# A fused two-block kernel: sparse attention's rotary half swap, by a TensorE permutation or by transfers within SBUF

## The chip, the cores and the metric

One Trainium2 chip, one core of it. The time is device microseconds of one execution of the whole program; lower is better. All arithmetic is in fp32 (with fp32r pairs for the large products).

## What is computed

The program runs a first block (two layers with a short convolution, a WKV recurrence and MLPs) and then a second block (sparse attention A, MLP, forgetting attention B, MLP) on 256 tokens of width 1024. The change touches sparse attention A alone:

```python
def apply_rope(x):                     # x: heads of 64
    half = d // 2
    x1, x2 = x[..., :half], x[..., half:]
    return concatenate([x1 * c - x2 * sn, x1 * sn + x2 * c], axis=-1)

def dsa_attention(xn, w_in, w_o):
    q, k, v, qi, ki, wi = split(xn @ w_in)
    q, k, qi, ki = (apply_rope(t) for t in (q, k, qi, ki))
    idx_logits = einsum('bqhd,bsd->bqhs', qi, ki)
    score = einsum('bqhs,bqh->bqs', relu(idx_logits), wi)      # admissible keys only
    sel = top_k(score, 64)
    logits = q @ k[sel] / 8;  o = softmax(logits) @ v[sel]
    return o @ w_o
```

## The kernel before

Everything is feature-major: 128 features on the partitions (two heads of 64), 256 tokens along the row. A large product is cut into weight units of 1 MB (1024 x 256, or 512 x 512 for the output weights). SP loads a unit into one of four `stage` buffers; ScalarE copies it to `w_hi` (fp32r), and VectorE or GpSimd subtracts to make `w_lo` (each in two halves, two buffers of each); TensorE then makes three products per tile (lines 2259 to 2261, or 2316 to 2318 for the wide units). SP's queue is one in-order list of transfers: the load of unit u waits until unit u-4 has both its `w_lo` halves (`lo_made`).

The units of attention A are numbered here from 0: 0 is the index key with its head weights, 1 and 2 the index queries, 3 the key, 4 the value, 5 to 8 the queries Q0 to Q3, 9 to 12 the output weights; after them come the units of the next MLP. `w_lo` of units 6, 7 and 8 is made by GpSimd (line 860, eight instructions each), that of the others by VectorE (line 1514).

The rotary embedding runs on eight results r = 0 to 7: the index key (one tile of 256 tokens), two index queries, the key, Q0 to Q3 (two tiles each). For each, ScalarE copies the unit's PSUM bank to `rope_in[r % 2]` (line 1366, which frees the bank, `un_free`). TensorE multiplies it with a 128 x 128 signed permutation `rot_w`, so that each half of a head comes to stand where the other was (lines 2781 and 2853); GpSimd makes the cosine product `rope_c` (line 850); VectorE makes the sine product from PSUM (line 2058) and adds `rope_c` (line 2060, `rope_done`). `rope_c` is one buffer, so GpSimd's cosine product of r waits for the sum of r-1.

The order on each engine is written out by hand. GpSimd's list has, after the rotary product of r = 3, 4 and 5, the subtraction of unit 6, 7 and 8, and each of these waits for the sum of that r (`rope_done`). VectorE's list is: index sums, scores(0), `w_lo` of unit 5, scores(1), the key's sum, half of the selection of 64 keys, Q0's sum, the other half of the selection, `sel_bias`, the first pair of heads' logits, Q1's sum, then a loop over eight pairs p with Q2's sum in p = 1 and Q3's in p = 3; `w_lo` of unit 9 is made in p = 2. TensorE's logits of pair p wait for the sum of Q(p // 2), from the fifth pair on (p >= 5) for all four sums.

Of the kernel before, what the change touches and what calls it, by code (L numbers as in the profile page):

```python
# [7 lines left out]
ALU = mybir.AluOpType  # L8
# [5 lines left out]
P = 128  # L14
# [6 lines left out]
HD = 64  # L21
# [27 lines left out]
CONST_PARTS = ((("ident", P), ("mean", P), ("ones", P), ("rot", P)),  # L49
# [13 lines left out]
def constant_table():  # L63
# [13 lines left out]
    rot = np.zeros((P, P))  # L77
    for m in range(P):
        d = m % HD
        rot[m + HD // 2 if d < HD // 2 else m - HD // 2, m] = -1.0 if d < HD // 2 else 1.0  # L80
    put("rot", rot)
# [11 lines left out]
    put("sin", np.tile(np.sin(ang), (4, 1)))  # L93
# [7 lines left out]
def build(nc, A, out):  # L101

    with ExitStack() as ctx:
# [65 lines left out]
        ident, mean_w, ones_w, head_ones, head_mean, rot_w = (c_(n) for n in ("ident", "mean", "ones", "head_ones", "head_mean", "rot"))  # L169
# [105 lines left out]
        rope_in = [at(f"rope_in{i}", [P, 2, SEQ], r_off[3] + 2048 * i) for i in range(2)]  # L275
        rope_c = at("rope_c", [P, 2, SEQ], r_off[3] + 4096)
# [185 lines left out]
        ROPE_KI, ROPE_QI, ROPE_K, ROPE_Q, N_ROPE = 0, 1, 3, 4, 8  # L462

# [164 lines left out]
        def _(sp):  # L628
# [29 lines left out]

            for k in range(ADA_FIRST):
                sp.dma_start(ada_buf[ada_slot(k)][:], ada_src(k)).then_inc(ada_first_landed[k], 16)  # L660
                if k == 0:
                    sp.dma_start(vec_in[:, 0:2, :], A["vec_table"][0:2 * P].rearrange("(t r) q -> r t q", r=P)).then_inc(vec_loaded, 16)
                    sp.dma_start(vec_in[0:N_VEC - 2 * P, 2, :], A["vec_table"][2 * P:]).then_inc(vec_loaded, 16)
                    sp.dma_start(const[0][:], A["const_table"][:, CONST_AT[0]:CONST_AT[1]]).then_inc(const_in, 16)
                if k == 1:
                    sp.dma_start(x[:], A["x"][0].rearrange("(a p) d -> p a d", p=P)).then_inc(x_loaded, 16)
            for u in range(NU):
# [59 lines left out]
        rot_done, rope_done, ki_copied, cos_done, kdup_ready = (sem(n) for n in ("rot_done", "rope_done", "ki_copied", "cos_done", "kdup_ready"))  # L727
# [9 lines left out]
        def _(pool):  # L737
# [107 lines left out]
            for r in range(N_ROPE):  # L845
                n = 1 if r == ROPE_KI else 2
                pool.wait_ge(un_free, freed(V_A + ROPE_USE[r]))
                if r:
                    pool.wait_ge(sem("rope_done"), r)
                G.tensor_tensor(rope_c[:, 0:n, :], rope_in[r % 2][:, 0:n, :], cos_root.unsqueeze(1).to_broadcast([P, n, SEQ]), ALU.mult)\  # L850
                    .then_inc(sem("cos_done"), 1)
# [640 lines left out]
        def _(dve):  # L1492
# [650 lines left out]
            dve.wait_ge(rot_done, ROPE_KI + 1)  # L2143
# [14 lines left out]
            def rope_query(j):  # L2158
                rope(ROPE_Q + j, 2, q_fm[:, 2 * j:2 * j + 2, :], un[(V_A + 5 + j) % 2])
# [3 lines left out]
            V.tensor_scalar(sel_bias[:], score[:], 0.5 * TAKEN, NEG, ALU.is_gt, ALU.mult).then_inc(sem("keys_chosen"), 1)  # L2163
            dve.wait_ge(sem("keys_chosen"), 1)
# [89 lines left out]
        def _(pe):  # L2254
# [630 lines left out]
            rot(ROPE_K, 2, V_A + 3)  # L2885
# [3 lines left out]
            rot_query(0)  # L2889
# [5 lines left out]
            rot_query(1)  # L2895
# [3 lines left out]
            for p in range(1, PAIRS):  # L2899
# [5 lines left out]
                if p in (1, 3):  # L2905
                    rot_query(p // 2 + 2)
# [128 lines left out]
```

## Time and profile before

| | us |
|---|---|
| median of 3 runs | 1351.86 (1350.39 to 1352.41) |
| the profiled execution: its own time | 1350.53 |
| its span, first to last instruction | 1348.8 |
| TensorE matmul busy | 1303.3 (97%) |
| VectorE busy | 948.8 (70%) |
| ScalarE busy | 701.5 (52%) |
| GpSimd busy | 128.3 (10%) |
| HBM, mean over the span | 189 GB/s |

Busy is the time in which an engine executed an instruction, added over the span. Attention A's projections and heads take the stretch from about 755 to 850 us. PE is TensorE, DVE VectorE, ACT ScalarE, POOL GpSimd, SPq the transfers that SP issues.

### The profile page before, as it was taken

What the parts mean: (1) busy time and instruction counts of PE and PEld (TensorE: products, weight loads), DVE (VectorE), ACT (ScalarE), POOL (GpSimd) and SP (SyncE); (2) the same over time, 40 slices, a digit from 0 to 9 for tenths busy, and PEclk for the clock granted to TensorE, in tenths of its full rate; (3) what the DMA queues carried; (4) which work ended last, traced back from release to release, by engine and by line L of the source; (5) the groups of instructions that cost most, each with busy time, mean ns of one, the idle gap of its engine ahead of it and who ended that gap; (6) DMA issues with size and microseconds to landing.
All of it is one profiled execution on the core that took longest, in us unless ns stands there. A gap on an engine that the chain in (4) does not pass through costs nothing. (4 is left out here: it accounts for less than half of the span.)

```text
span 1348.8 us, 24952 instructions
## 1 busy us (share of the span) xinstructions
PE 1303.3 (97%) x10507; PEld 1129.8 (84%) x10507; DVE 948.8 (70%) x1433; ACT 701.5 (52%) x1211; POOL 128.3 (10%) x133
## 2 busy tenths in 40 slices
PE   4999999999999999999999999999999999999997
PEld 2998888998899897788888887888888998888886
DVE  1887788976768776675566888666656677756655
ACT  2544544434567555564444648654445566644443
POOL 0000000010200764100000042000000021000000
PEclk9999999999999999999999999999999999999999
DMA  9996799995341012356665532465555543565561
GB/s 362 372 363 237 299 356 380 352 343 167 115 156 64 4 35 97 95 176 201 188 189 176 182 113 91 148 206 192 187 190 160 174 139 126 172 188 194 183 197 50
DMA packets 177575, 256.90 MB, mean 190 GB/s; under 512 B 10488, under 2 KB 122552, under 8 KB 177464
## 3 DMA queue, kind: packets, MB, share of 16 engines
q1 hardware_dynamic: 177464, 255.31, 56.8%
q8 instruction: 83, 1.36, 0.4%
q14 instruction: 28, 0.23, 0.1%
HBM read 254.25 MB, written 1.05 MB: 189 GB/s over the span
## 5 line engine op out<-in xcount | busy, mean ns | idle before, releaser
L1514 DVE TENSOR_TENSOR w_lo<-stage,w_hi 128x1024 fp32r<-128x1024 f32 (+1 forms) x372 | 447.6, 1239 | 160.4 <-ACT w_hi L889 160.0
L889 ACT ACTIVATE w_hi<-stage 128x1024 fp32r<-128x1024 f32 (+1 forms) x378 | 380.1, 1049 | 211.7 <-PE acc L2318 191.9
L2316 PE MATMUL acc<-w_hi,z_hi 128*128 128x512 f32 x640 | 252.6, 395 | 1.6 <-DVE z_lo L1963 1.6
L2318 PE MATMUL acc<-w_hi,z_lo 128*128 128x512 f32 x640 | 249.4, 390 | 0.0
L2317 PE MATMUL acc<-w_lo,z_hi 128*128 128x512 f32 x640 | 249.2, 389 | 0.0
L2259 PE MATMUL un<-h_both,w_hi 128*128 128x256 f32 x736 | 214.3, 291 | 1.8 <-POOL w_lo L860 1.1
L2260 PE MATMUL un<-h_both,w_hi 128*128 128x256 f32 x736 | 208.1, 283 | 0.0
L2261 PE MATMUL un<-h_both,w_lo 128*128 128x256 f32 x736 | 208.0, 283 | 0.0
L2259 PEld LDWEIGHTS un<-h_both,w_hi 128*128 128x128 f32 x736 | 140.8, 191 | 9.5 <-issue 5.4
L2316 PEld LDWEIGHTS acc<-w_hi,z_hi 128*128 128x128 f32 x640 | 120.1, 188 | 27.8 <-issue 4.0
L2260 PEld LDWEIGHTS un<-h_both,w_hi 128*128 128x128 f32 x736 | 141.0, 192 | 1.2 <-issue 0.7
L2318 PEld LDWEIGHTS acc<-w_hi,z_lo 128*128 128x128 f32 x640 | 120.1, 188 | 25.4
L2261 PEld LDWEIGHTS un<-h_both,w_lo 128*128 128x128 f32 x736 | 140.9, 191 | 0.0
L2317 PEld LDWEIGHTS acc<-w_lo,z_hi 128*128 128x128 f32 x640 | 120.3, 188 | 23.5
L2297 PE MATMUL un<-h_both,w_hi 128*128 128x512 f32 x384 | 121.2, 397 | 0.4 <-DVE w_lo L1514 0.4
L2297 PE MATMUL side<-h_both,w_hi 128*128 128x512 f32 x384 | 120.8, 396 | 0.4
L2300 PEld LDWEIGHTS side<-h_both,w_lo 128*128 128x128 f32 x384 | 72.1, 188 | 17.0
L2300 PEld LDWEIGHTS un<-h_both,w_lo 128*128 128x128 f32 x384 | 72.1, 188 | 16.9
L2300 PE MATMUL un<-h_both,w_lo 128*128 128x256 f32 x384 | 75.5, 278 | 0.0
L2300 PE MATMUL side<-h_both,w_lo 128*128 128x256 f32 x384 | 75.4, 278 | 0.0
L1796 DVE SCALAR_TENSOR_TENSOR ada_sum<-ada_buf,small,ada_sum 128x1024 f32<-128x1024 f32 x49 | 62.8, 1282 | 1.0
L2297 PEld LDWEIGHTS un<-h_both,w_hi 128*128 128x128 f32 x384 | 59.1, 189 | 1.6 <-DVE w_lo L1514 0.6
(393 smaller groups left out, 1886.0 us busy)
## 6 DMA issues: line engine op xcount, KB each, us to landing
stage<-in_mlp_w SPq DMA_DIRECT2D x64, 1024.0 KB
ada_buf<-in_ada_w SPq DMA_DIRECT2D x48, 1024.0 KB, 11.4
stage<-in_w_up SPq DMA_DIRECT2D x32, 1024.0 KB
stage<-in_w_down SPq DMA_DIRECT2D x32, 1024.0 KB
stage<-in_conv_w_in SPq DMA_DIRECT2D x12, 1024.0 KB
stage<-in_rw_w_rkv SPq DMA_DIRECT2D x12, 1024.0 KB
stage<-in_w_in_a SPq DMA_DIRECT2D x8, 1024.0 KB
stage<-in_w_kv_b SPq DMA_DIRECT2D x8, 1024.0 KB
```

What stands on the lines that cost most here:

```text
L889: A_(w_hi[u % 2][:, half, 0:n], stage[u % NSTAGE][:, half, 0:n], ACT.Copy).then_inc(hi_made, 1)
L1514: V.tensor_tensor(w_lo[u % 2][:, half, 0:n], stage[u % NSTAGE][:, half, 0:n], w_hi[u % 2][:, half, 0:n].bitcast(F32), ALU.subtract).then_i ...
L1796: V.scalar_tensor_tensor(out=to[:], in0=rows, scalar=by, in1=to[:], op0=ALU.mult, op1=ALU.add).then_inc(ada_weighed, 1)
L2259: MM(out, hi_l, hi_r, start=start, stop=False, skip_group_check=True)
L2260: MM(out, hi_l, lo_r, start=False, stop=False, skip_group_check=True)
L2261: return MM(out, lo_l, hi_r, start=False, stop=stop, skip_group_check=True)
L2297: MM(pair[:, m, :, :], wh[:, kt, c], h_both[:, kt, :, :], start=(kt == 0), stop=False, skip_group_check=True)
L2300: ins = MM(pair[:, m, 0, :], wl[:, kt, c], h_hi[:, kt, :], start=False, stop=(kt == KT - 1), skip_group_check=True)
L2316: MM(y, z_hi[:, kt, q], wh[:, i, :], start=(first and kt == 0), stop=False, skip_group_check=True)
L2317: MM(y, z_hi[:, kt, q], wl[:, i, :], start=False, stop=False, skip_group_check=True)
L2318: ins = MM(y, z_lo[:, kt, q], wh[:, i, :], start=False, stop=(last and kt == KT - 1), skip_group_check=True)
```

## The change

The half swap is no longer made by TensorE. SP issues, for each r, four transfers from `rope_in` to a new buffer `rope_turned[r % 2]` of 32 partitions each, block 0 to 1, 1 to 0, 2 to 3 and 3 to 2, as soon as `rope_in` is there. GpSimd makes the cosine product and behind it the sine product in place on `rope_turned`; the sign is in the sine table now. VectorE only adds the two. The eight permutation products, the wait of TensorE's later units for the sums, and the separate semaphore behind `sel_bias` are gone. The new buffer lies in the second half of `tmp`.

In SP's list the swaps stand at fixed places, each ahead of one weight load: r = 0 to 3 ahead of the loads of units 6 to 9, r = 4 ahead of unit 11, r = 5 ahead of unit 12, r = 6 and 7 ahead of the next MLP's first and second unit (`SWAPPED_AHEAD`).

```diff
-    put("sin", np.tile(np.sin(ang), (4, 1)))
+    put("sin", np.tile(np.sin(ang), (4, 1)) * np.where(i % HD < HD // 2, -1.0, 1.0)[:, None])
...
+        rope_turned = [at(f"rope_turned{i}", [P, 2, SEQ], tmp_off + 4096 + 2048 * i) for i in range(2)]
...
+        SWAPPED_AHEAD = (U_KI + 6, U_KI + 7, U_KI + 8, U_KI + 9, U_QA + 6, U_QA + 7, U_OA + 4, U_OA + 5)
...
+            def swap_halves(r):
+                n = 1 if r == ROPE_KI else 2
+                sp.wait_ge(un_free, freed(V_A + ROPE_USE[r]))
+                for g in range(4):
+                    to, src = 32 * g, 32 * (g ^ 1)
+                    sp.dma_start(rope_turned[r % 2][to:to + 32, 0:n, :], rope_in[r % 2][src:src + 32, 0:n, :]).then_inc(sem(f"rope_landed{r % 2}"), 16)
...
+                if u in SWAPPED_AHEAD:
+                    swap_halves(SWAPPED_AHEAD.index(u))
                 load_unit(u)
...
-                G.tensor_tensor(rope_c[:, 0:n, :], rope_in[r % 2][:, 0:n, :], cos_root.unsqueeze(1).to_broadcast([P, n, SEQ]), ALU.mult)\
-                    .then_inc(sem("cos_done"), 1)
+                G.tensor_tensor(rope_c[:, 0:n, :], rope_in[r % 2][:, 0:n, :], cos_root.unsqueeze(1).to_broadcast([P, n, SEQ]), ALU.mult)
+                pool.wait_ge(sem(f"rope_landed{r % 2}"), 64 * (r // 2 + 1))
+                turned = rope_turned[r % 2][:, 0:n, :]
+                G.tensor_tensor(turned, turned, sin_root.unsqueeze(1).to_broadcast([P, n, SEQ]), ALU.mult).then_inc(sem("cos_done"), 1)
...
-            def rope(r, n, dst, bank=misc):
-                dve.wait_ge(rot_done, r + 1)
-                link(V.tensor_tensor(dst, bank[:, 0:n, :], bc4(sin_root, n), ALU.mult))
+            def rope(r, n, dst):
                 dve.wait_ge(cos_done, r + 1)
-                V.tensor_tensor(dst, dst, rope_c[:, 0:n, :], ALU.add).then_inc(rope_done, 1)
+                V.tensor_tensor(dst, rope_turned[r % 2][:, 0:n, :], rope_c[:, 0:n, :], ALU.add).then_inc(rope_done, 1)
...
-            def rot(r, n, v):
-                pe.wait_ge(un_free, freed(v))
-                if r:
-                    pe.wait_ge(rope_done, r)
-                MM(misc[:, 0:n, :], rot_w, rope_in[r % 2][:, 0:n, :], start=True, stop=True).then_inc(rot_done, 1)
...
             def a_unit(k, tokens=False):
                 free_bank(V_A + k)
-                if k >= 7:
-                    pe.wait_ge(rope_done, ROPE_Q + k - 6)
...
-            def rot_query(j):
-                v = V_A + 5 + j
-                pe.wait_ge(un_free, freed(v))
-                MM(un[v % 2][:], rot_w, rope_in[(ROPE_Q + j) % 2][:], start=True, stop=True).then_inc(rot_done, 1)
```

How the lists stand around the queries. SP's list before, from the load of unit 8 (the first row) over units 9 to 12 to the first two units of the next MLP:

```order
L644 DMA stage_49<-in_w_in_a 128x8x256 [waits lo_made]
L644 DMA stage_50<-in_w_o_a 128x4x512 [waits lo_made]
L644 DMA stage_51<-in_w_o_a 128x4x512 [waits lo_made]
L644 DMA stage_52<-in_w_o_a 128x4x512 [waits lo_made]
L644 DMA stage_49<-in_w_o_a 128x4x512 [waits lo_made]
L644 DMA stage_50<-in_w_up 128x8x256 [waits lo_made]
L644 DMA stage_51<-in_w_up 128x8x256 [waits lo_made]
```

And now, from the load of unit 10 to the last swap (Q0 to Q3 are `rope_in_161`, `162`, `161`, `162`):

```order
L641 DMA stage_51<-in_w_o_a 128x4x512 [waits lo_made]
L662 DMA rope_turned_163<-rope_in_161 32x512 [waits un_free]
L662 DMA rope_turned_163<-rope_in_161 32x512 x3
L641 DMA stage_52<-in_w_o_a 128x4x512 [waits lo_made]
L662 DMA rope_turned_164<-rope_in_162 32x512 [waits un_free]
L662 DMA rope_turned_164<-rope_in_162 32x512 x3
L641 DMA stage_49<-in_w_o_a 128x4x512 [waits lo_made]
L662 DMA rope_turned_163<-rope_in_161 32x512 [waits un_free]
L662 DMA rope_turned_163<-rope_in_161 32x512 x3
L641 DMA stage_50<-in_w_up 128x8x256 [waits lo_made]
L662 DMA rope_turned_164<-rope_in_162 32x512 [waits un_free]
L662 DMA rope_turned_164<-rope_in_162 32x512 x3
```

Each swap of a query stands directly behind a weight load: Q0's behind unit 10, Q1's behind unit 11, Q2's behind unit 12, Q3's behind the next MLP's first unit, and these four loads wait for `w_lo` of units 6, 7, 8 and 9.

GpSimd's list before, from Q0's cosine product over the subtraction of unit 7 to Q1's:

```order
L850 TENSOR_TENSOR rope_c<-rope_in_161,rstd 128x512 [waits rope_done,un_free]
L860 TENSOR_TENSOR w_lo_56<-stage_52,w_hi_54 128x256 [waits hi_made,lo_made,rope_done]
L860 TENSOR_TENSOR w_lo_56<-stage_52,w_hi_54 128x256 x3
L860 TENSOR_TENSOR w_lo_56<-stage_52,w_hi_54 128x256 [waits hi_made]
L860 TENSOR_TENSOR w_lo_56<-stage_52,w_hi_54 128x256 x3
L850 TENSOR_TENSOR rope_c<-rope_in_162,rstd 128x512 [waits rope_done,un_free]
```

And the same stretch now:

```order
L857 TENSOR_TENSOR rope_c<-rope_in_161,rstd 128x512 [waits rope_done,un_free]
L860 TENSOR_TENSOR rope_turned_163<-rope_turned_163,rstd 128x512 [waits rope_landed0]
L869 TENSOR_TENSOR w_lo_56<-stage_52,w_hi_54 128x256 [waits hi_made,lo_made,rope_done]
L869 TENSOR_TENSOR w_lo_56<-stage_52,w_hi_54 128x256 x3
L869 TENSOR_TENSOR w_lo_56<-stage_52,w_hi_54 128x256 [waits hi_made]
L869 TENSOR_TENSOR w_lo_56<-stage_52,w_hi_54 128x256 x3
L857 TENSOR_TENSOR rope_c<-rope_in_162,rstd 128x512 [waits rope_done,un_free]
L860 TENSOR_TENSOR rope_turned_164<-rope_turned_164,rstd 128x512 [waits rope_landed1]
```

The sine product has joined the cosine product, with a wait for the swap's landing between them; the subtraction of the weight unit stands behind both, as it stood behind the one.

## Rows read from the trace of the kernel before

**Rows 1.** the page, its part on busy time per engine
```profile
PE 1303.3 (97%) x10507; PEld 1129.8 (84%) x10507; DVE 948.8 (70%) x1433; ACT 701.5 (52%) x1211; POOL 128.3 (10%) x133
```

**Rows 2.** windows (us; busy us of each engine with instruction counts; TensorE clock; DMA)
```profile
795.00:810.00 15.00, 14.31 (x108) 12.28 (x108) 13.80 (x45) 8.04 (x13) 11.23 (x15) 1.00 0.40 133
...
830.00:840.00 10.00, 10.00 (x78) 7.62 (x78) 8.41 (x18) 8.73 (x27) 0.00 (x0) 1.00 0.01 2
```

**Rows 3.** timeline of PE: start, duration, line, operands; the second rotary product
```profile
771.49 0.28 PE L2261 MATMUL un<-h_both,w_lo 128*128 128x256 f32 x1
771.61 1.02 PE L2781 MATMUL side<-rope_in,const 128*128 128x512 f32 x2
...
772.59 0.28 PE L2260 MATMUL un<-h_both,w_hi 128*128 128x256 f32 x1
```

**Rows 4.** timeline of DVE; in brackets the idle time before, its releaser
```profile
773.40 0.69 DVE L2060 TENSOR_TENSOR qi_fm<-qi_fm,rope_c 128x512 f32<-128x512 f32 x1
774.01 3.43 DVE L1514 TENSOR_TENSOR w_lo<-stage,w_hi 128x1024 fp32r<-128x1024 f32 x2
...
786.85 0.48 DVE L2123 SCALAR_TENSOR_TENSOR score<-score_r,wi_tok,const 128x256 f32<-128x256 f32 x1 [0.37 <-ACT score_r L1385]
...
791.75 0.69 DVE L2060 TENSOR_TENSOR kA_fm<-kA_fm,rope_c 128x512 f32<-128x512 f32 x1
...
799.48 0.69 DVE L2060 TENSOR_TENSOR q_fm<-q_fm,rope_c 128x512 f32<-128x512 f32 x1 [0.68 <-POOL rope_c L850]
...
819.20 0.69 DVE L2060 TENSOR_TENSOR q_fm<-q_fm,rope_c 128x512 f32<-128x512 f32 x1
...
822.51 2.35 DVE L1514 TENSOR_TENSOR w_lo<-stage,w_hi 128x1024 fp32r<-128x1024 f32 x2
...
828.22 0.69 DVE L2060 TENSOR_TENSOR q_fm<-q_fm,rope_c 128x512 f32<-128x512 f32 x1
```

**Rows 5.** the rotary products on POOL: min/median/max ns, first and last start
```profile
L850 POOL TENSOR_TENSOR rope_c<-rope_in,rstd x8: 746/1285/2122, 769.8 to 826.4; 128x512 f32<-128x512 f32 x7, 128x256 f32<-128x256 f32 x1
```

**Rows 6.** timeline of POOL
```profile
774.23 2.12 POOL L850 TENSOR_TENSOR rope_c<-rope_in,rstd 128x512 f32<-128x512 f32 x1 [1.68 <-DVE qi_fm L2060]
...
792.53 5.59 POOL L860 TENSOR_TENSOR w_lo<-stage,w_hi 128x256 fp32r<-128x256 f32 x8 [11.31 <-DVE kA_fm L2060]
```

**Rows 7.** timeline of SP's queue, one of the weight loads
```profile
798.15 0.39 SPq L644 DMA_DIRECT2D stage<-in_w_o_a  x1
```

**Rows 8.** who SP's queue waited for, 755 to 850 us: total, times, longest
```profile
SPq L644 <- POOL w_lo L860: 29.0, 3, 11.2
```

**Rows 9.** windows of the load issued at 798.15 us, DMA share and GB/s last
```profile
801.70:802.70 1.00, 1.00 (x11) 0.87 (x10) 0.96 (x6) 0.11 (x1) 1.00 (x2) 1.00 0.89 344
802.70:803.70 1.00, 1.00 (x11) 0.67 (x10) 0.93 (x5) 0.98 (x2) 1.00 (x2) 1.00 0.03 10
```

**Rows 10.** tiles: four 32-partition pieces of lora_g2b, and the output's four
```profile
L681 SPq DMA_DIRECT2D lora_g2b<-in_rw_g x4: 417/421/429, 335.9 to 337.3; - x4
...
DMA to landing us min/median/max: 3.9/4.1/4.4
...
DMA to landing us min/median/max: 2.0/2.1/2.1
```

**Rows 11.** timeline of PE, the index scores and the logits of the fifth pair
```profile
779.15 1.16 PE L2838 MATMUL acc<-ki_fm,qi_fm 64*128 64x128 f32 x16
...
828.96 0.93 PE L2792 MATMUL un<-k_dup,q_fm 64*128 64x128 f32 x8 [0.43 <-DVE q_fm L2060]
```

**Rows 12.** PE near the start of the run, one timeline row and three windows
```profile
16.20 0.91 PE L2326 MATMUL acc<-const,xs_sq 128*128 128x128 f32 x3 [7.23 <-DVE xs_sq L1537]
...
20.60:22.80 2.20, 2.20 (x25) 1.06 (x28) 0.00 (x0) 0.00 (x0) 0.00 (x0) 1.00 1.03 411
22.80:25.00 2.20, 2.20 (x28) 1.06 (x24) 0.00 (x0) 0.00 (x0) 0.00 (x0) 1.00 1.03 410
25.00:27.20 2.20, 2.20 (x48) 1.23 (x44) 0.00 (x0) 0.38 (x1) 0.00 (x0) 1.00 1.01 399
```

More of the change, by code:

```diff
@@ L45 @@
            "c", "final_g", "g_attn_a_2", "g_kv_2", "g_attn_b_2", "g_mlp_2", "g_final_2")
-CONST_PARTS = ((("ident", P), ("mean", P), ("ones", P), ("rot", P)),
+CONST_PARTS = ((("ident", P), ("mean", P), ("ones", P), ("still", P)),
                (("head_ones", P), ("head_mean", P), ("level_t", 6 * CHUNK), ("masks", 2 * CHUNK), ("eye", CHUNK), ("resets", SEQ),
@@ L76, in constant_table @@
     put("head_mean", same_head / HD)
[L77 to L81, printed above, removed]
     s, q = i[:, None] % CHUNK, np.arange(CHUNK)[None, :]
@@ L167, in c_ @@
             return const[i][:, lo - CONST_AT[i]:hi - CONST_AT[i]]
-        ident, mean_w, ones_w, head_ones, head_mean, rot_w = (c_(n) for n in ("ident", "mean", "ones", "head_ones", "head_mean", "rot"))
+        ident, mean_w, ones_w, head_ones, head_mean = (c_(n) for n in ("ident", "mean", "ones", "head_ones", "head_mean"))
         level_t = c_("level_t").rearrange("p (j q) -> p j q", j=6)
@@ L726, in build @@
                              "bonus_gated", "weighed", "scaled", "group_done", "last_done"))
-        rot_done, rope_done, ki_copied, cos_done, kdup_ready = (sem(n) for n in ("rot_done", "rope_done", "ki_copied", "cos_done", "kdup_ready"))
+        wi_turned, rope_done, ki_copied, cos_done, kdup_ready = (sem(n) for n in ("wi_turned", "rope_done", "ki_copied", "cos_done", "kdup_ready"))
         score_done, score_relu, score_used = sem("score_done"), sem("score_relu"), sem("score_used")
@@ L2142, in _ @@
             dve.wait_ge(tables_made, 1)
-            dve.wait_ge(rot_done, ROPE_KI + 1)
+            dve.wait_ge(wi_turned, 1)
             for a in range(QT):
@@ L2158, in rope_query @@
             def rope_query(j):
-                rope(ROPE_Q + j, 2, q_fm[:, 2 * j:2 * j + 2, :], un[(V_A + 5 + j) % 2])
+                rope(ROPE_Q + j, 2, q_fm[:, 2 * j:2 * j + 2, :])
             rope_query(0)
             select(rounds - rounds // 2)
-            V.tensor_scalar(sel_bias[:], score[:], 0.5 * TAKEN, NEG, ALU.is_gt, ALU.mult).then_inc(sem("keys_chosen"), 1)
-            dve.wait_ge(sem("keys_chosen"), 1)
+            link(V.tensor_scalar(sel_bias[:], score[:], 0.5 * TAKEN, NEG, ALU.is_gt, ALU.mult))
             pair_logits(0, 0)
@@ L2844, in a_half @@
                     free_bank(V_A + k)
-                    if k >= 7:
-                        pe.wait_ge(rope_done, ROPE_Q + k - 6)
                 unit(U_KI + k, un[(V_A + k) % 2], h_tiles, tokens=tokens, kts=HALVES[n])
-            def rot_query(j):
-                v = V_A + 5 + j
-                pe.wait_ge(un_free, freed(v))
-                MM(un[v % 2][:], rot_w, rope_in[(ROPE_Q + j) % 2][:], start=True, stop=True).then_inc(rot_done, 1)
             def a_products(p):
@@ L2874, in _ @@
             for a in range(QT):
-                nc.tensor.transpose(misc[:, 1, IDX_HEADS * a:IDX_HEADS * (a + 1)], rope_in[ROPE_KI % 2][HD:KI_COLS, 0, P * a:P * a + P],
+                ins = nc.tensor.transpose(misc[:, 1, IDX_HEADS * a:IDX_HEADS * (a + 1)], rope_in[ROPE_KI % 2][HD:KI_COLS, 0, P * a:P * a + P],
                                     ident[HD:KI_COLS, HD:KI_COLS])
-            rot(ROPE_KI, 1, V_A)
+            ins.then_inc(wi_turned, 1)
             a_unit(2)
-            rot(ROPE_QI, 2, V_A + 1)
             a_half(3, 0)
-            rot(ROPE_QI + 1, 2, V_A + 2)
             a_half(3, 1)
@@ L2884, in _ @@
             a_half(4, 0, tokens=True)
-            rot(ROPE_K, 2, V_A + 3)
             index_scores(1)
@@ L2888, in _ @@
             a_unit(5)
-            rot_query(0)
             a_unit(6)
@@ L2894, in _ @@
             a_half(7, 0)
-            rot_query(1)
             a_products(1)
@@ L2904, in _ @@
                 pair_turns(0, p - 1)
-                if p in (1, 3):
-                    rot_query(p // 2 + 2)
                 if p in (1, 2):
```

## The prediction

> **What bounds the kernel now.** The page's first part says that TensorE is the bound over the whole span: 1303.3 us busy, 97% [rows 1]. The change sits in one stretch, so the windows come next. From 795 to 810 us, where the keys are selected and Q0 and Q1 are turned, PE is busy 14.31 of 15 us and VectorE 13.80; from 830 to 840 PE is busy 10.00 of 10 [rows 2]. So a microsecond taken from TensorE is gained only where nothing else is late, and any lateness that reaches 830 us is carried to the end, for from there PE has no gap to lose it in. Third, the timelines of VectorE, GpSimd and SP tell who is right behind whom. Q0's sum waited 0.68 us for GpSimd's product [rows 4]; the logits of pair p = 5 started at 828.96 after 0.43 us of waiting for Q3's sum [rows 11], which ends at 828.22 + 0.69 = 828.91 [rows 4]. The rotary sums are thus already at the edge of the path. Fourth, SP: its queue waited 29.0 us, three times, for GpSimd's `w_lo` [rows 8]. The load at 798.15 [rows 7] is that of unit 10, and it went out when GpSimd had ended unit 6, at 792.53 + 5.59 = 798.12 [rows 6].
>
> **What the change takes away.** TensorE: the second product started at 771.61, 0.12 us behind the product before it, and the second instruction behind it started at 772.59 instead of 771.61 + 0.12 [rows 3]: 0.86 us for two tiles. Seven of them are 6.0 us; the eighth, of one tile, is half of that and stands ahead of a wait, I put it at nothing. VectorE loses eight multiplications of the size of its sums, seven by 0.69 us [rows 4]. GpSimd gains eight products: 0.75 us for the index key, 1.29 for the others [rows 5], some 9.7 us. It is nearly idle over the span, but serial: cosine, sine, sum, next cosine.
>
> **The index part and the key.** Here the swaps have room, since they stand ahead of loads, behind ones that went out early. What counts is GpSimd. Before, the first index query's sum ended at 773.40 + 0.69 = 774.09 [rows 4]. Now the index key's costs 0.75 more, then come two products and a sum, and it ends near 775.3, 1.2 us later. Then the second index query's two products (2.6 us) run beside VectorE's `w_lo` (2.35 us when alone [rows 4]). They do not overlap: before, one product took 2.12 there instead of 1.29 [rows 5, 6], and `w_lo` 3.43 instead of 2.35 [rows 4], so that both together took about their sum. That makes 4.9 us instead of 3.4, less the multiplication of 0.7, so 2 us late in all. The index scores, at 779.15 before [rows 11], start near 781.1, and the three products that TensorE was spared by then (under 2.2 us) become waiting. VectorE's second part of the scores had 0.37 us of idle time ahead [rows 4] and the key's multiplication behind, which absorb 1.1: the key's sum, before at 791.75 + 0.69 = 792.44 [rows 4], ends near **793.2**. Bounds: 791.7, if only the multiplication goes, and 793.9, if nothing is absorbed but that.
>
> **The queries: a loop through four engines.** This is the term that decides. In SP's list Q0's swap stands behind the load of unit 10, which waits for GpSimd's `w_lo` of unit 6; that waits for the key's sum. Q1's swap stands behind unit 11's load, which waits for `w_lo` of unit 7, which waits for Q0's sum; and so on. Before, TensorE turned the halves off this loop. Now each turn of it is: sum, subtraction, load, swap, sine product, next sum. The subtraction takes 5.6 us [rows 6]. The load and the swap, call it L, are counted from the load's issue to the landing of the fourth piece. The load's data filled the engines until about 802.7 (share 0.89 until then, 0.03 after), 4.6 us after its issue, at up to some 400 GB/s [rows 7, 9]. The swap's 256 KB queue behind it on the same engines: 0.65 us at that rate, and a little for the landing, so L = 5.4. Lower bound: the pieces overtake the load and cost their issue, 0.39 + 4 x 0.42, and a landing as that of the output, 2.1 [rows 7, 10]: 4.2. Upper bound: the four 32-partition pieces of `lora_g2b`, queued behind other loads, took up to 4.4 to land [rows 10]; 0.39 + 1.7 + 4.4 is 6.5. I take 5.4, near the middle, for the order of the queue. The sine product is 1.29, the sum 0.69, four handoffs some 0.3 (792.44 to 792.53 is one [rows 4, 6]). A turn is 5.6 + 5.4 + 1.3 + 0.7 + 0.3 = **13.3 us**. Before, the sums of the queries lay 9 to 10 us apart, Q2's to Q3's 9.0 [rows 4].
> Q0 ends at 793.2 + 13.3 = 806.5 (before 799.48 + 0.69 = 800.17 [rows 4]), Q1 at 819.8, Q2 at 833.1 (before 819.89). For Q3 the load in front waits for `w_lo` of unit 9, which VectorE makes 822.51 + 2.35 - 819.89 = 4.97 us after Q2's sum [rows 4]: 833.1 + 4.97 + 5.4 + 1.3 + 0.7 + 0.3 = **845.8**, against 828.91. Pair 5's logits follow at once, 16.8 us late, and from there TensorE has no gap [rows 2], so the end is as late.
>
> **What else hides or shows.** The 6.0 us that TensorE is spared lie before 829 and become waiting. While VectorE waits for Q0's sum, its second half of the selection, `sel_bias` and all logits queue behind it; behind SP's queue waits stand weight loads, but those go out before their swap, and the units they bring are wanted later by as much as the rest. SP's 32 issues of 0.42 us fit in its waits. The swaps' 1.9 MB are under 5 us of the DMA engines, at under half load there [rows 2].
> **The sum:** bounds for four L are -4.8 and +4.4, for the start -1.5 and +0.7, so 16.8 with 10.5 to 21.9. On the profiled execution's 1350.53 us that is 1367.3; the median shown lies 1.33 above it, so **1368.7 us**.
> By the Trainium skill, "DMA: Bandwidth & Descriptors", section "Anatomy of one DMA", a transfer costs about 2.0 us and its bytes at 436 GB/s; with nothing in front that is 2.6 us for a swap, and as an estimate the kernel would then lose some 6 us instead of 16.8. The same page ("Queues, rings and completion order") has each engine take descriptors in the order of its ring, which speaks for the longer L; no row before shows two such transfers behind one another within SBUF.
>
> **Rivals.**
> *Clock.* TensorE waits long now: some 4.5 us for Q0's sum, and 5 to 7 for Q2's and Q3's. Near the start, after an idle 7.23 us, 25 and then 28 matmuls ran in 2.2 us where later 48 did [rows 12]: half the rate, 1.2 instead of 2.4 GHz, for about 4.4 us, a loss of 2.0 us (4.4 - 53/48 x 2.2). The column of granted clock says 1.00 there, against it. Falls before 829 us are hidden in waits, the one before pair 5's logits is not: +2.0, **1370.7**. Chance 0.28. The Trainium skill, "TensorE: Matmul & The Clock Gate", section "What's actually happening", has the clock fall to half when the engine has been idle, which would be this; by it the estimate is the same.
> *Short loop.* The pieces go out and land together within 2.1 us of the load's issue and its 0.39 [rows 7, 10]: L = 2.5, four times 2.9 less, +5.2: **1357.1**. Against it: four issues alone take 1.7 us. Chance 0.08.
> *Faster.* TensorE keeps all 6.0 us: 1351.86 - 6.0 = **1345.9**. That needs Q0's operands before VectorE comes to its sum at 799.48 - 0.68 = 798.8; the load of unit 10 goes out at 798.15 with the swap behind it, so L and 1.3 us of product would have to fit in about 0.65 us. It decides for the change only if the swaps do not really wait behind the loads. Chance 0.04.
> The forecast has 0.58; 0.02 is left for balance around no change.
>
> **The numbers.** The forecast's bounds give 1362.4 to 1373.8, with the clock up to 1375.8. The range reaches a little toward the short loop: 1360 to 1376. About 0.2% (2.7 us) is what a measurement can tell from no change here: faster 0.04, same 0.02, slower 0.94.
>
> **What would show it.** SP's queue: each query swap issued directly after the loads of units 10, 11, 12 and the next one, its landing 5 to 6 us after the load's issue. GpSimd: sine products waiting for a DMA. VectorE: some 7 us idle ahead of Q0's sum, sums 13 us apart ending near 806, 820, 833 and 846. TensorE: waits for the `q_fm` sums, and busy time some 6 us or more lower at an unchanged clock. VectorE's busy time falls by about 5 us, GpSimd's rises by about 10. Wrong, if the distance of the sums stays at 9 to 10 us, if the swaps are issued before the loads' waits end, or if TensorE catches up after 830 us.

## Result and profile after

The changed kernel takes 1379.12 us (median of 5 runs, 1377.06 to 1380.40) against 1350.39 us for the kernel before (5 runs, 1349.95 to 1352.41): a ratio of 1.0207, interval 1.0196 to 1.0218. It is 28.7 us slower, where 16.8 were forecast, and 3.1 us above the range. The profiled execution took 1379.27 us with a span of 1377.4; that of before had 1348.8.

First, the busy time of each engine from the page of the changed kernel, to be held against [rows 1]:

```profile
PE 1307.2 (95%) x10491; PEld 1137.1 (83%) x10491; DVE 944.6 (69%) x1425; ACT 701.9 (51%) x1211; POOL 138.6 (10%) x141
```

VectorE lost 4.2 us, GpSimd gained 10.3: as forecast. TensorE did not get 6 us cheaper but 3.9 dearer, without its eight permutation products. The windows say why (columns as in [rows 2], PE alone):

```profile
795.00:810.00 15.00, 10.01 (x84) 0.93 0.31 98
810.00:820.00 10.00, 8.25 (x45) 0.60 0.23 79
...
830.00:840.00 10.00, 5.98 (x49) 0.84 0.43 134
...
850.00:860.00 10.00, 6.38 (x38) 0.66 0.14 40
860.00:870.00 10.00, 10.00 (x84) 1.00 0.14 30
```

In the kernel before every one of these stretches up to 850 us has a granted clock of 1.00. Here it is 0.60 to 0.93 (0.74 from 820 to 830, 0.73 from 840 to 850). TensorE is idle for a third of the time up to 850 us, and after each long wait it works for a few microseconds at 1.2 GHz instead of 2.4 (the first logits behind such a wait take 1.65 us instead of 0.93). Only from 860 us on is it full and fast.

VectorE's timeline gives the key's sum and the four query sums (start, length, line; in brackets the idle time ahead and what ended it), which answer to [rows 4]:

```profile
795.28 0.69 DVE L2067 TENSOR_TENSOR kA_fm<-rope_turned,rope_c 128x512 f32<-128x512 f32 x1
...
809.70 0.69 DVE L2067 TENSOR_TENSOR q_fm<-rope_turned,rope_c 128x512 f32<-128x512 f32 x1 [8.10 <-POOL rope_turned L860]
...
824.36 0.69 DVE L2067 TENSOR_TENSOR q_fm<-rope_turned,rope_c 128x512 f32<-128x512 f32 x1 [4.78 <-POOL rope_turned L860]
...
840.23 0.69 DVE L2067 TENSOR_TENSOR q_fm<-rope_turned,rope_c 128x512 f32<-128x512 f32 x1 [8.94 <-POOL rope_turned L860]
...
853.75 0.69 DVE L2067 TENSOR_TENSOR q_fm<-rope_turned,rope_c 128x512 f32<-128x512 f32 x1 [5.39 <-POOL rope_turned L860]
```

They end at 795.97, 810.39, 825.05, 840.92 and 854.44, so 14.4, 14.7, 15.9 and 13.5 us apart, where the forecast had 13.3 three times and 12.7. GpSimd and SP, for one turn of the loop (Q0) and for its third (Q2):

```profile
796.05 5.62 POOL L869 TENSOR_TENSOR w_lo<-stage,w_hi 128x256 fp32r<-128x256 f32 x8 [6.20 <-DVE kA_fm L2067]
...
808.34 1.26 POOL L860 TENSOR_TENSOR rope_turned<-rope_turned,rstd 128x512 f32<-128x512 f32 x1 [5.41 <-DMA rope_turned<-rope_in]
...
838.94 1.26 POOL L860 TENSOR_TENSOR rope_turned<-rope_turned,rstd 128x512 f32<-128x512 f32 x1 [6.74 <-DMA rope_turned<-rope_in]
```

```profile
801.69 0.40 SPq L641 DMA_DIRECT2D stage<-in_w_o_a  x1
802.13 2.42 SPq L662 DMA_DIRECT2D rope_turned<-rope_in  x4
...
830.98 0.40 SPq L641 DMA_DIRECT2D stage<-in_w_o_a  x1
831.42 4.08 SPq L662 DMA_DIRECT2D rope_turned<-rope_in  x4
...
848.14 2.41 SPq L662 DMA_DIRECT2D rope_turned<-rope_in  x4
```

The key's sum ends at 795.97; GpSimd makes `w_lo` of unit 6 until 801.67; SP issues the load of unit 10 at 801.69 and the four pieces of the swap behind it (2.42 us, in place of the 1.7 I counted); the sine product starts at 808.34, having waited 5.41 us for the transfer. So L, from the load's issue to the landing, is 6.65 us here. In the second turn it is 7.0 and in the third 8.0, where the four issues took 4.08 us. The last swap (848.14) waited not for the load, which SP had issued at 845.80, but for `rope_in`, whose copy on ScalarE had waited for TensorE's product. It landed 4.3 us after its own issue, 6.7 us after the load's.

**Where 28.6 us of span come from.** The sum in four stretches, each from two rows of the timelines. The start is ScalarE's first copy into `rope_in`, 762.97 us before and 764.19 after.

| stretch | before | after | more | forecast |
|---|---|---|---|---|
| up to the first `rope_in` | 762.97 | 764.19 | 1.2 | 0 |
| from there to the key's sum | 29.47 | 31.78 | 2.3 | 0.8 |
| key's sum to Q3's sum | 36.47 | 58.47 | 22.0 | 16.1 |
| Q3's sum to the end of the span | 519.89 | 522.96 | 3.1 | 0 |

Up to the first `rope_in` the work is the same; in the 12 kernels below that point lies anywhere from 762.1 to 764.8. I take the 1.2 us for scatter of single executions.

### The profile page after: what moved, and what is told of

Read it like the earlier page. It is cut to its first block, busy times and chain, and to the rows that moved or that the text cites. A ratio compares the mean times of both kernels' runs of the same rounds, so it can differ in the third digit from the quotient of the medians.

```text
span 1377.4 us, 24941 instructions
## 1 busy us (share of the span) xinstructions
PE 1307.2 (95%) x10491; PEld 1137.1 (83%) x10491; DVE 944.6 (69%) x1425; ACT 701.9 (51%) x1211; POOL 138.6 (10%) x141
## 4 chain that ended last, share of the span: by engine, by line
PE 83%; DVE 7%; DMA 2%; POOL 2%; issue 2%; ACT 2%; SPq 1%; DVEq 0%; ACTq 0%; POOLq 0%
PE acc L2322 11%; PE acc L2324 10%; PE acc L2323 10%; PE un L2265 7%; PE un L2266 7%; PE un L2267 7%; PE side L2303 7%; PE un L2303 6%; PE side L2306 3%; PE un L2306 3%; PE acc L2655 2%; DVE w_lo L1523 2%; PE side L2655 2%; DMA stage<-in_conv_w_in 2%; POOL w_lo L869 1%
## 5 line engine op out<-in xcount | busy, mean ns | idle before, releaser
L2265 PEld LDWEIGHTS un<-h_both,w_hi 128*128 128x128 f32 x736 | 143.1, 194 | 10.5 <-issue 6.9
L2266 PEld LDWEIGHTS un<-h_both,w_hi 128*128 128x128 f32 x736 | 143.2, 195 | 0.5
L2306 PEld LDWEIGHTS un<-h_both,w_lo 128*128 128x128 f32 x384 | 72.1, 188 | 16.9
L1805 DVE SCALAR_TENSOR_TENSOR ada_sum<-ada_buf,small,ada_sum 128x1024 f32<-128x1024 f32 x49 | 62.8, 1282 | 1.0
L2303 PEld LDWEIGHTS un<-h_both,w_hi 128*128 128x128 f32 x384 | 59.1, 189 | 1.6 <-DVE w_lo L1523 0.6
```

The lines of the kernel that those rows point to most:

```text
L1805: V.scalar_tensor_tensor(out=to[:], in0=rows, scalar=by, in1=to[:], op0=ALU.mult, op1=ALU.add).then_inc(ada_weighed, 1)
L2265: MM(out, hi_l, hi_r, start=start, stop=False, skip_group_check=True)
L2266: MM(out, hi_l, lo_r, start=False, stop=False, skip_group_check=True)
L2303: MM(pair[:, m, :, :], wh[:, kt, c], h_both[:, kt, :, :], start=(kt == 0), stop=False, skip_group_check=True)
L2306: ins = MM(pair[:, m, 0, :], wl[:, kt, c], h_hi[:, kt, :], start=False, stop=(kt == KT - 1), skip_group_check=True)
```

## Experiments

All start from the changed kernel. The three columns of stretches are those of the table above, from one profiled execution each; before and after for comparison.

| kernel | median us | ratio to before, interval | start to key | key to Q3 | Q3 to end |
|---|---|---|---|---|---|
| before | 1350.39 | | 29.5 | 36.5 | 519.9 |
| after | 1379.12 | 1.0207 (1.0196 to 1.0218) | 31.8 | 58.5 | 523.0 |
| swaps one load earlier | 1364.26 | 1.0095 (1.0080 to 1.0110) | 31.4 | 44.0 | 523.5 |
| swap in front of its load | 1369.04 | 1.0131 (1.0116 to 1.0146) | 31.7 | 49.8 | 523.8 |
| queries on TensorE | 1353.88 | 1.0022 (1.0012 to 1.0031) | 32.5 | 36.5 | 519.8 |
| index and key on TensorE | 1376.13 | 1.0191 (1.0174 to 1.0207) | 29.5 | 59.0 | 522.4 |
| ScalarE issues the swaps | 1375.18 | 1.0182 (1.0166 to 1.0198) | 37.6 | 48.1 | 522.9 |
| eight pieces a swap | 1382.54 | 1.0235 (1.0217 to 1.0253) | 32.0 | 62.8 | 522.3 |
| `w_lo` on VectorE | 1369.00 | 1.0135 (1.0120 to 1.0150) | 32.2 | 49.7 | 522.4 |
| earlier swaps and `w_lo` on VectorE | 1366.41 | 1.0114 (1.0099 to 1.0129) | 32.3 | 47.9 | 522.0 |
| sine product on VectorE | 1373.19 | 1.0174 (1.0153 to 1.0195) | 29.9 | 55.7 | 522.2 |
| unread matmuls, 12 8 13 8 | 1385.55 | 1.0253 (1.0238 to 1.0268) | 31.9 | 62.9 | 524.7 |
| unread matmuls, 6 4 6 3 | 1378.79 | 1.0212 (1.0196 to 1.0228) | 32.5 | 57.6 | 521.0 |
| unread matmuls, 6 4 8 4 | 1376.63 | 1.0187 (1.0172 to 1.0202) | 31.8 | 58.6 | 522.5 |

**Is it the loop? Swaps one load earlier.** One line changes, the place in SP's list:

```diff
-SWAPPED_AHEAD = (..., U_QA + 6, U_QA + 7, U_OA + 4, U_OA + 5)
+SWAPPED_AHEAD = (..., U_QA + 5, U_QA + 6, U_QA + 7, U_OA + 4)
```

> The four query swaps stand one weight load earlier in SyncE's list (ahead of the loads of units 10, 11, 12 and of the MLP's first unit), so that none waits for GpSimd's w_lo any more; the rest is the changed kernel. Loop theory (the loss is the chain sum, w_lo, load, swap, sine, sum): the swap is over before the sine product wants it, a query costs w_lo 5.6 + cosine 1.3 + sine 1.3 + sum 1.0 = 9.2 us or the projection's own time, the last query sum ends near 834 us instead of 854.4, and the median is 1359 (1355 to 1363). Rival (the transfers are slow by themselves, wherever they stand): 1373 to 1379.

Measured 1364.26, a little over the loop theory's 1355 to 1363 and 9 us below the rival's: half of the loss was the order of one queue. SP and GpSimd of this kernel, in the turns of Q1 and Q3:

(Line numbers are those of each kernel's own file.)

```profile
803.50 2.41 SPq L662 DMA_DIRECT2D rope_turned<-rope_in  x4
810.18 0.40 SPq L641 DMA_DIRECT2D stage<-in_w_o_a  x1
...
831.95 2.41 SPq L662 DMA_DIRECT2D rope_turned<-rope_in  x4
```

```profile
811.35 1.41 POOL L860 TENSOR_TENSOR rope_turned<-rope_turned,rstd 128x512 f32<-128x512 f32 x1
...
835.85 1.26 POOL L860 TENSOR_TENSOR rope_turned<-rope_turned,rstd 128x512 f32<-128x512 f32 x1 [2.58 <-DMA rope_turned<-rope_in]
```

Q1's swap goes out at 803.50, 6.7 us before the load of unit 11, and its sine product waits for nothing (those of Q0 and Q2 still waited 1.7 and 1.3 us). Q3's swap (831.95) now follows its copy at once, and still the product starts at 835.85, 3.9 us after the issue. That latency, with 1.26 us of product, stands in place of a product on TensorE that took 0.86 [rows 3]. It is what I had left out of 1359; where the copy itself comes late, the order of the queue does not take it away.

**What is L made of? The swap in front of its load, behind the same wait.**

```diff
-                if u in SWAPPED_AHEAD:
+                if u + 1 in SWAPPED_AHEAD[4:]:
+                    sp.wait_ge(lo_made, 2 * (u - NSTAGE + 1))
+                    swap_halves(SWAPPED_AHEAD.index(u + 1))
+                if u in SWAPPED_AHEAD[:4]:
                     swap_halves(SWAPPED_AHEAD.index(u))
```

> Each query swap is issued behind the same wait for w_lo, but ahead of the 1 MB weight load instead of behind it. Sharing theory (the 1.3 to 2.6 us by which the swap was late beyond its own pieces is the load in the same queue): from the load's place to the landing 4 us instead of 6.7 to 8.0, some 3 us less per query, median 1367 (1364 to 1370). Rival (the swap's own issues and landings make the whole time, the load takes only its issue of 0.4 us): 1.3 us less per query at most, median 1374 to 1378.

Measured 1369.04, inside the sharing theory's range. SP and GpSimd:

```profile
800.05 2.41 SPq L662 DMA_DIRECT2D rope_turned<-rope_in  x4
802.50 0.60 SPq L641 DMA_DIRECT2D stage<-in_w_o_a  x1
```

```profile
804.00 1.27 POOL L863 TENSOR_TENSOR rope_turned<-rope_turned,rstd 128x512 f32<-128x512 f32 x1 [2.71 <-DMA rope_turned<-rope_in]
```

From the swap's first issue to the sine product it is 3.95 us here, and 3.91 and 4.17 in the second and third turn; behind the load it was 6.65, 7.0 and 8.0. The megabyte in front costs a swap 2.7, 3.1 and 3.8 us, its own issue being 0.40 of that; in the third turn part of the 3.8 are the slow issues (4.08 us, here 2.65).

**Does the number of issues count? Eight pieces instead of four,** the same bytes; GpSimd's wait counts the additional ones:

```diff
-                    sp.dma_start(rope_turned[r % 2][to:to + 32, 0:n, :], ...)
+                    for m in (slice(0, 1), slice(1, 2)) if r >= ROPE_Q else (slice(0, n),):
+                        sp.dma_start(rope_turned[r % 2][to:to + 32, m, :], ...)
```

> The changed kernel with each query swap cut into eight transfers of 32 KB instead of four of 64 KB, the same bytes. Issue theory (SyncE's 0.6 us an issue stands in the loop): 2.4 us more per query, the query sums some 17 us apart, median 1389 (1386 to 1392). Rival (bytes beside the weight load set the landing, issues are covered): 1379 to 1382.

Measured 1382.54, 3.4 us more than after: neither theory's number. The rows tell the two cases apart:

```profile
817.21 0.39 SPq L641 DMA_DIRECT2D stage<-in_w_o_a  x1
817.65 5.19 SPq L663 DMA_DIRECT2D rope_turned<-rope_in  x8
...
850.41 4.94 SPq L663 DMA_DIRECT2D rope_turned<-rope_in  x8
```

```profile
824.79 1.26 POOL L861 TENSOR_TENSOR rope_turned<-rope_turned,rstd 128x512 f32<-128x512 f32 x1 [6.36 <-DMA rope_turned<-rope_in]
...
856.71 1.26 POOL L861 TENSOR_TENSOR rope_turned<-rope_turned,rstd 128x512 f32<-128x512 f32 x1 [4.97 <-DMA rope_turned<-rope_in]
```

With the load directly in front, L goes from 6.65, 7.0 and 8.0 to 7.85, 7.6 and 7.9 us: most of the 2.5 us of additional issues lies beside the load's data. With `rope_in` late and the load gone ahead (850.41), the swap takes 6.3 us instead of 4.3: there 2.0 of the 2.5 us count.

**Is `w_lo` in the loop? VectorE makes it for units 6 to 8 too,** in a `split` behind the key's sum and the first two query sums.

```diff
-                if r in (ROPE_K, ROPE_Q, ROPE_Q + 1):
+                if False:
...
             rope(ROPE_K, 2, kA_fm[:])
+            split(U_QA + 1)
...
             rope_query(0)
+            split(U_QA + 2)
...
             rope_query(1)
+            split(U_QA + 3)
```

> The changed kernel, but VectorE makes w_lo of units 6, 7 and 8 too, right behind the key's sum and the first two query sums, in 2.35 us instead of GpSimd's 5.6; swaps and loads keep their order. Loop theory (w_lo stands between a sum and the next load and swap): 3.2 us less three times, from the key's sum to the last query sum 49 us instead of 58.5, median 1369.5 (1367.5 to 1372). Rival (VectorE's own list is then the bound, or the swap of the last query hangs on TensorE anyway): 1374 to 1380.

Measured 1369.00, as the loop theory has it: a shorter link of the chain shortens the kernel, though it puts 6 us on VectorE (busy 950.5 us instead of 944.6). Turn by turn the theory fits only the first two, 2.7 and 2.6 us shorter. The third is 5.1 shorter and the fourth 1.6 longer, and in both the swap waited for `rope_in` and no longer for the load. Together with the earlier swaps:

> Both at once: swaps one load earlier in SyncE's list, and VectorE makes w_lo of units 6 to 8. With the swaps one load earlier alone TensorE still waited 1.9 us for w_lo and GpSimd for late swaps. Loop theory: from the key's sum to the last query sum 40 us instead of 44.0, median 1360 (1357 to 1362). Rival (7 us more on VectorE are paid in full): 1365 to 1371.

Measured 1366.41, in the rival's range and, if anything, slower than the earlier swaps alone (1364.26; the two intervals overlap). VectorE and GpSimd between the sums of Q0 and Q1:

```profile
806.47 3.44 DVE L1523 TENSOR_TENSOR w_lo<-stage,w_hi 128x1024 fp32r<-128x1024 f32 x2
...
817.95 0.68 DVE L2067 TENSOR_TENSOR q_fm<-rope_turned,rope_c 128x512 f32<-128x512 f32 x1
```

```profile
809.76 1.30 POOL L860 TENSOR_TENSOR rope_turned<-rope_turned,rstd 128x512 f32<-128x512 f32 x1 [0.94 <-DMA rope_turned<-rope_in]
```

Q1's turned half is ready at 811.06 and its sum starts at 817.95: `w_lo` (3.44 us beside GpSimd's cosine product), half of the selection and the first logits stand ahead in VectorE's list. With the swap out of the way, VectorE is the bound.

**Queries or index part?** First the queries on TensorE (as before the change), the rest by swap; then the reverse. Both restore a permutation table, the product and VectorE's two operations for the results concerned, the first also TensorE's waits for the query sums; of the first kernel:

```diff
-                if u in SWAPPED_AHEAD:
+                if u in SWAPPED_AHEAD[:4]:
...
             a_unit(5)
+            rot_query(0)
             a_unit(6)
...
+                link(V.tensor_tensor(dst, un[(V_A + 5 + j) % 2][:], bc4(sin_root, 2), ALU.mult))
+                dve.wait_ge(cos_done, ROPE_Q + j + 1)
+                V.tensor_tensor(dst, dst, rope_c[:], ALU.add).then_inc(rope_done, 1)
```

> The four query results are turned by TensorE's product with a permutation, as before, and GpSimd makes only their cosine product; the index key, the index queries and the key keep the swap by transfers. Loop theory: the queries make nearly the whole loss; what stays is the key's sum, 2.3 us later than before in the trace, median 1353 (1351 to 1356). Rival (the index part costs as much, through VectorE and GpSimd getting in each other's way): 1358 to 1365.

> The reverse of the run that turned the queries on TensorE: index key, index queries and key on TensorE as before, the four queries by swap. If the two parts of the loss add up, this one gives back what that one still lost (3.6 us): 1375.5 (1373.5 to 1377.5). Rival (the parts hide one another, the query loop alone sets the end whenever it begins): 1378 to 1380.

Measured 1353.88 and 1376.13, both as the first theory has it. Swapping only the index and key results loses 3.6 us against the runs of before beside it, swapping only the queries 26.0: together 29.6, about the 28.7 of both. The first is the nearest that any variant comes to the kernel before.

**Where does the key lose 2.3 us? The sine product back on VectorE,** from `rope_turned`, ahead of the sum; GpSimd makes the cosine product alone.

```diff
+                dve.wait_ge(sem(f"rope_landed{r % 2}"), 64 * (r // 2 + 1))
+                link(V.tensor_tensor(dst, rope_turned[r % 2][:, 0:n, :], bc4(sin_root, n), ALU.mult))
                 dve.wait_ge(cos_done, r + 1)
-                V.tensor_tensor(dst, rope_turned[r % 2][:, 0:n, :], rope_c[:, 0:n, :], ALU.add).then_inc(rope_done, 1)
+                V.tensor_tensor(dst, dst, rope_c[:, 0:n, :], ALU.add).then_inc(rope_done, 1)
```

> The changed kernel with the sine product on VectorE again, straight from rope_turned, GpSimd making only the cosine product. Loop theory: 1.27 us of GpSimd become 0.7 of VectorE in each query's chain, 0.6 us four times, and GpSimd's two products no longer follow one another in the index part, 1 us: median 1376 (1374 to 1378). Rival (the products' place is of no account beside the swap): 1378 to 1380.

Measured 1373.19, below the range of both: more than I gave it. The table says where: the key's sum comes 29.9 us after the start instead of 31.8, nearly the 29.5 of before. The changed kernel's timelines of the index part show how GpSimd's second product meets VectorE, twice:

```profile
777.57 2.12 POOL L857 TENSOR_TENSOR rope_c<-rope_in,rstd 128x512 f32<-128x512 f32 x1 [0.87 <-DVE qi_fm L2067]
779.65 2.24 POOL L860 TENSOR_TENSOR rope_turned<-rope_turned,rstd 128x512 f32<-128x512 f32 x1
...
788.48 1.36 POOL L860 TENSOR_TENSOR rope_turned<-rope_turned,rstd 128x512 f32<-128x512 f32 x1 [4.46 <-DMA rope_turned<-rope_in]
```

```profile
787.50 3.43 DVE L1523 TENSOR_TENSOR w_lo<-stage,w_hi 128x1024 fp32r<-128x1024 f32 x2
```

The second index query's cosine and sine products take 2.12 and 2.24 us instead of 1.3 beside a `w_lo` of 3.43 instead of 2.35; that was forecast. The second meeting at 787.5 was not: the key's sine product, late for its transfer, falls on VectorE's next `w_lo` and stretches that to 3.43 as well. But that alone does not hold up the key. In the kernel with the swaps one load earlier this `w_lo` took 2.36 us, VectorE then waited for the index scores, and the key still came 31.4 us after the start:

```profile
785.33 2.36 DVE L1523 TENSOR_TENSOR w_lo<-stage,w_hi 128x1024 fp32r<-128x1024 f32 x2
...
788.92 0.48 DVE L2130 SCALAR_TENSOR_TENSOR score<-score_r,wi_tok,const 128x256 f32<-128x256 f32 x1 [1.23 <-ACT score_r L1394]
```

The scores are late because TensorE makes their second part late. Its two parts in the changed kernel with the window between them, then with the sine product on VectorE:

```profile
782.76 1.16 PE L2836 MATMUL acc<-ki_fm,qi_fm 64*128 64x128 f32 x16 [4.01 <-DVE qi_fm L2067]
...
788.42 2.00 PE L2836 MATMUL acc<-ki_fm,qi_fm 64*128 64x256 f32 x16
```

```profile
784.00:786.00 2.00, 2.00 (x10) 0.50 1.16 369
```

```profile
779.78 1.16 PE L2836 MATMUL acc<-ki_fm,qi_fm 64*128 64x128 f32 x16 [2.73 <-DVE qi_fm L2067]
...
783.93 2.00 PE L2836 MATMUL acc<-ki_fm,qi_fm 64*128 64x256 f32 x16
```

From the first part to the second it is 5.66 us behind a wait of 4.01, with the granted clock down to 0.50, and 4.15 us behind a wait of 2.73, where the clock stayed at 1.00. In the kernel before it was 5.03 (779.15 to 784.18) with the key's permutation product of 0.86 in between, so 4.17 without it. The fall of the clock costs TensorE 1.5 us here. In the changed kernel the slow TensorE and the stretched `w_lo` release VectorE within 0.2 us of one another. The run with the earlier swaps shows that the first holds up the key without the second; the sine product on VectorE takes both away, and no run takes away the first alone.

**Another queue: ScalarE issues the swaps** behind its own copies.

```diff
-                if u in SWAPPED_AHEAD:
-                    swap_halves(SWAPPED_AHEAD.index(u))
...
                 A_(rope_in[r % 2][:, 0:n, :], ...).then_inc(un_free, 1)
+                act.wait_ge(un_free, freed(V_A + ROPE_USE[r]))
+                for g in range(4):
+                    ...
+                    act.dma_start(rope_turned[r % 2][to:to + 32, 0:n, :], ...)
```

> All eight swaps are issued by ScalarE, right behind its own copy into rope_in, none by SyncE. Order theory (SyncE's list is what makes the swap late): swaps no longer wait for w_lo nor follow a 1 MB load in its queue; four issues of 0.6 us are added to ScalarE eight times; last query sum near 838 us, median 1363 (1358 to 1368). Rival (a swap of 256 KB takes 6 us and more in any queue): 1371 or more.

Measured 1375.18: a miss of the expected number, in the rival's range for another reason than the rival's. From the key to Q3 it is 48.1 us, 10 less, as the order theory says. But from the start to the key it is 37.6, 5.8 more:

```profile
764.90 3.55 ACTq L1377 DMA_DIRECT2D rope_turned<-rope_in  x4
768.55 2.00 ACT L896 ACTIVATE w_hi<-stage 128x1024 fp32r<-128x1024 f32 x2 [3.69 <-issue]
```

ScalarE spends 3.55 us with four issues while the next `w_hi`, for which VectorE then waited 4.22 us, stands behind them. Here an issue is cheap only on an engine whose list has nothing urgent in it.

**What does the clock cost?** Matmuls on the identity whose result nobody reads, ahead of TensorE's four long waits. Of the third of these kernels:

```diff
+            keep_warm(V_A + 7, 6)
...
+                if p == 1:
+                    keep_warm(V_A + 8, 4)
+                if p == 4:
+                    keep_warm(V_A + 9, 4)
...
+                if p == 2:
+                    keep_warm(V_A + 9, 8)
```

> The changed kernel with 12, 8, 13 and 8 matmuls of 512 columns on the identity, whose result nobody reads, ahead of TensorE's four long waits between 804 and 854 us. Clock theory (part of the loss is that TensorE works at half rate after each wait): the granted clock of 805 to 862 us stays near 1.0, pair 5's logits take 0.93 us and not 1.65, the median is 1375.5 (1374 to 1377.5). Rival (the waits are set by the other engines alone, and work between them has room to spare): 1379, within 1 us; if the matmuls stand in the way, above it.

> As the run before it with unread matmuls, but with 6, 4, 6 and 3 of them: in that run one took 0.85 us, so that 12 of them lasted twice as long as the wait that they stood in. Now they fill 5.1, 3.4, 5.1 and 2.6 us of waits of 5.5, 3.7, 5.9 and 3.6 us. Clock theory: the granted clock of 810 to 860 us is near 1.0 and the median is 1375 (1373.5 to 1377.5). Rival (the half rate after the waits costs nothing, since the other engines set the time): 1378 to 1380.

> The unread matmuls again, now 6, 4, 8 and 4 (5.1, 3.4, 6.8 and 3.4 us), so that less of the third and fourth wait stays open. In the trace of the run before, the stretch behind the last query sum was 2.0 us shorter than in the changed kernel, and the way there 0.9 us shorter, yet the median moved by 0.3. Clock theory: the granted clock is 1.0 from 840 us on and the median is 1376.5 (1375 to 1377.8). Rival: 1378.2 to 1380.

The first misjudged one such matmul by a factor of two (0.85 us, not the 0.43 that I read from an earlier place; the trace counts two matmuls for each): the clock was 1.00 from 795 to 870 us, but the products stood behind the fillers, and it took 1385.55. The second kernel, at 1.00 with two dips to 0.87 and 0.79 between 820 and 840, took 1378.79 (its rival's number), the third 1376.63 (its theory's). The intervals of both overlap with that of the changed kernel, so the medians alone do not settle it. The rows behind the last wait do; first the changed kernel, then the second filler kernel (PE, pair 5's logits, then pair 6's):

```profile
854.50 1.65 PE L2792 MATMUL un<-k_dup,q_fm 64*128 64x128 f32 x8 [3.57 <-DVE q_fm L2067]
...
860.44 0.93 PE L2792 MATMUL un<-k_dup,q_fm 64*128 64x128 f32 x8
```

```profile
854.79 0.93 PE L2792 MATMUL un<-k_dup,q_fm 64*128 64x128 f32 x8 [1.54 <-DVE q_fm L2067]
...
858.65 0.93 PE L2792 MATMUL un<-k_dup,q_fm 64*128 64x128 f32 x8
```

From pair 5's logits to pair 6's it is 5.94 us at first half and then full rate, and 3.86 with the clock kept up; in the kernel before it was 3.86 too (828.96 to 832.82). 2.1 of the 3.1 us behind Q3's sum are the clock. In the third filler kernel this last wait was 1.85 us instead of 1.54, the logits took 1.29 us and the distance 5.42: the filler did not hold there.

The other 1.0 us lies behind VectorE's last instruction, which starts 2.07 us later after Q3's sum than before. The last output transfer landed 3.1 us after its issue, against at most 2.1 before [rows 10]:

```profile
DMA to landing us min/median/max: 2.1/2.1/3.1
```

The second filler kernel has the same 3.1, the one with the sine product on VectorE 2.1. No run ties this to the swap, and I leave its cause open.

## Why the prediction was right in kind and short in size

**Right:** the direction and the mechanism. The query swaps stand in a loop through four engines: moving them in the list, moving them past the load, and shortening `w_lo` each took 10 to 15 us off, and taking the queries out of it left 3.6. (The fourth turn closed over TensorE's late product and `rope_in`, which the forecast did not have.) GpSimd's and VectorE's busy times, the order of events in each turn and the collision of GpSimd with VectorE's `w_lo` in the index part came as written. *Short loop* and *Faster* did not occur. The range ended at 1376; the result is 3.1 above.

**Short, term by term** (11.7 us in the spans, 16.9 forecast and 28.6 measured):
- *L = 5.4 us* was the step that failed. It measured 6.65, 7.0, 8.0 and 6.7 us, all four above even the upper bound of 6.5, and together 6.7 us more than forecast. I had the order of the queue and the bytes at 400 GB/s right, but allowed next to nothing between the last byte and the product. In the first turn the DMA engines fell idle at 807.2, 5.5 us after the load's issue where I had 4.6 + 0.65, and the product began at 808.34, 1.1 us later:

```profile
806.20:807.20 1.00, 1.00 0.94 262
807.20:808.20 1.00, 0.80 0.02 4
```

  That is nearly the whole miss of this turn. In the third, the four issues took 4.08 us where I had 1.7. In the fourth, the swap went out 1.95 us after the load's issue had ended (845.80 + 0.39), because `rope_in` was late. An issue of a piece measured 0.60 us and not 0.42, but directly behind a load little of that shows (the run with eight pieces). The other links came out 0.8 us shorter over the four turns, so that the stretch to Q3 is 5.9 over.
- *The key's sum*, forecast 0.8 us late with an upper bound of 1.5, was 2.3 late. The second index query's sum was 2.6 us late where I had 2.0; "here the swaps have room" was not so, for GpSimd waited 0.98 us for the first index query's swap. Then TensorE's second part of the index scores, of which the sum says nothing, was 3.0 us late: the clock fell after a wait of 4.01 us (1.5 us), and at the same place VectorE's `w_lo` was stretched. The sine product on VectorE gives 1.9 us of it back.
- *The clock* was written as a rival with +2.0 us and a chance of 0.28, and it came true in addition: 2.1 us behind Q3's sum. Its sentence that falls before 829 us are hidden in waits failed in the index part. What spoke against it, the clock column of [rows 12], said less than the spacing of the matmuls there. The Trainium skill, "TensorE: Matmul & The Clock Gate", section "What's actually happening", has the clock fall when the engine idles; the windows after (0.60 to 0.84) agree.
- 1.0 us is the late landing of the last output transfer, cause open.
- 1.2 us are the different start of the two profiled executions, which I take for scatter.
- *TensorE's busy time* was forecast 6 us lower "at an unchanged clock". The clock was not unchanged, so that sentence could not be read off the busy time; a lower count of matmuls (10491 for 10507) and a lower clock meet in it.

By the figures of "DMA: Bandwidth & Descriptors", section "Anatomy of one DMA", in the Trainium skill a swap alone would have been 2.6 us; the trace has 3.9 with nothing in front, 2.4 of it issue time on the queue, which that estimate has not. The Trainium skill gives those figures for transfers issued from GpSimd, and these are issued by SP. Its sentence on the order of the ring (section "Queues, rings and completion order") agrees with the 2.7 us and more that the load in front costs.

No variant with a swap beats the kernel before. The nearest, with the queries on TensorE, is at a ratio of 1.0022; the best with all swaps at 1.0095.

## What to carry over

A transfer that replaces 0.9 us of a busy engine costs here 3.9 us of latency at best, and inherits the waits and the megabyte that stand ahead of it in its queue. Before moving work off the bounding engine into a DMA, write out who waits for whom once around: if the queue's own wait depends on the result, latency is paid at every turn. Waiting that it puts on TensorE is paid a second time where the clock falls and the next engine waits for the result (1.5 and 2.1 us here). And take the place in the list as part of the change: one line of it was worth 15 us.

## What the hardware did that I had not expected

- One issue of a 32-partition piece within SBUF takes SP 0.60 us, against 0.40 for a load of 1 MB; in the third turn four took 4.08 us instead of 2.4, and in the kernels with the index part on TensorE and with the sine product on VectorE 4.12 and 3.93 at the same place. A load issued directly behind a swap takes 0.60 too (802.50 above). I have no cause for either.
- The length of a wait alone does not tell at what rate TensorE goes on. After 1.54 us the logits took 0.93 us (second filler kernel), after 1.85 us 1.29 (third), and in the kernel with the sine product on VectorE 0.93 after 3.46 us; there the granted clock fell behind them, to 0.63 from 822 to 824 us:

```profile
821.09 0.93 PE L2792 MATMUL acc<-k_dup,q_fm 64*128 64x128 f32 x8 [3.46 <-DVE pair_logit L2082]
```

- A GpSimd product and a VectorE subtraction at the same time both take longer: 1.3 becomes 2.1 to 2.2, and 2.35 becomes 3.43.
